# Moving every activation buffer of a two-block transformer kernel 32 bytes down in SBUF

## The reference

```python
def first_block(x, mem, ...):
    memn = rmsnorm(mem, mem_norm)
    for l in range(2):
        h = rmsnorm(x, mix_norm[l])
        x = x + (ab_mixer(h, ...) if l == 0 else c_mixer(h, ...))
        x = x + mem_cross_attn(rmsnorm(x, xa_norm[l]), memn, ...)
        x = x + jnp.square(jax.nn.relu(rmsnorm(x, mlp_norm[l]) @ w1[l])) @ w2[l]
    return rmsnorm(x, final_norm)

def second_block(x, positions, ...):
    for l in range(2):
        h = rmsnorm_2(x, attn_norm[l])
        x = x + (even_attention(h) if l == 0 else moba_attention(h)) @ w_out
        x = x + conv_glu_ffn(rmsnorm_2(x, ffn_norm[l]), ...)
    return rmsnorm_2(x, final_norm)
```

## The kernel before

| buffer | bytes | starts at | modulo 512 |
|---|---|---|---|
| `ring_hi` | 24576 | 0 | 0 |
| `ring` / `ring_lo` | 24576 | 24576 | 0 |
| `consts` | 14636 | 49152 | 0 |
| `smalls` | 6924 | 63808 | 320 |
| `stream_margin` | 352 | 70752 | 96 |
| `xT` | 8192 | 71104 | 448 |

## Time and profile before

### The profile page before, as it was taken

The page is one execution under the profiler, slowest core; times in us unless marked ns, Lnnn a source line. Parts: engine busy times, 40 slices in busy tenths (PEclk is TensorE's granted clock), DMA queues, the critical chain, the costliest instruction groups (busy, mean ns, idle before and its releaser), DMA issues. The chain is left out here.

```text
span 1622.5 us, 32581 instructions
## 1 busy us (share of the span) xinstructions
PE 1558.7 (96%) x12614; PEld 1487.9 (92%) x12614; DVE 730.4 (45%) x1386; ACT 830.8 (51%) x1250; POOL 1183.6 (73%) x920
## 2 busy tenths in 40 slices
PE   7989999999999898999999999999999999999997
PEld 6978989999998788998999998889999997899997
DVE  6554644220187566544422015856553234465511
ACT  5663555554455553545555445465445444654442
POOL 5655966999977500596799897718989896389994
PEclk9999999999999899999999999999999999999999
DMA  7333534555544200353455553415555553255552
GB/s 276 133 104 104 195 118 165 192 195 191 193 166 148 102 1 2 106 194 117 169 193 193 194 189 130 155 47 176 188 189 183 181 195 118 77 172 189 187 183 103
DMA packets 67662, 248.04 MB, mean 153 GB/s; under 512 B 7632, under 2 KB 7888, under 8 KB 67152
## 3 DMA queue, kind: packets, MB, share of 16 engines
q1 hardware_dynamic: 67536, 246.19, 43.7%
HBM read 245.11 MB, written 1.05 MB: 152 GB/s over the span
## 5 line engine op out<-in xcount | busy, mean ns | idle before, releaser
L345 POOL TENSOR_TENSOR ring_lo<-ring,ring_hi 128x512 fp32r<-128x512 f32 x916 | 1183.4, 1330 | 419.6 <-ACT ring_hi L1004 417.4
L1004 ACT ACTIVATE ring_hi<-ring 128x1024 fp32r<-128x1024 f32 x458 | 466.1, 1052 | 200.8 <-DMA ring<-panels 192.7
L379 PE MATMUL ps_dve<-x_hi,ring_hi 128*128 128x256 f32 x1928 | 465.6, 281 | 16.9 <-POOL ring_lo L345 11.0
L379 PE MATMUL ps_dve<-x_lo,ring_hi 128*128 128x256 f32 x1928 | 461.3, 279 | 0.0
L379 PEld LDWEIGHTS ps_dve<-x_hi,ring_hi 128*128 128x128 f32 x1928 | 364.0, 189 | 22.8 <-issue 15.5
L379 PEld LDWEIGHTS ps_dve<-x_lo,ring_hi 128*128 128x128 f32 x1928 | 364.2, 189 | 0.5 <-issue 0.2
L379 PE MATMUL ps_dve<-x_hi,ring_lo 128*128 128x256 f32 x1928 | 274.1, 279 | 0.2
L379 PEld LDWEIGHTS ps_dve<-x_hi,ring_lo 128*128 128x128 f32 x1928 | 246.1, 189 | 0.9 <-POOL ring_lo L345 0.8
L379 PE MATMUL ps_dve<-work_parts,ring_hi 128*128 128x256 f32 x1728 | 228.7, 278 | 0.0
L379 PEld LDWEIGHTS ps_dve<-work_parts,ring_hi 128*128 128x128 f32 x1728 | 214.5, 188 | 0.0
L1492 DVE TENSOR_TENSOR xT<-xT,ps_dve 128x512 f32<-128x512 f32 x40 | 27.5, 687 | 318.9 <-PE ps_dve L379 318.8
(11 more groups left out here) (287 smaller groups left out, 1958.8 us busy)
## 6 DMA issues: line engine op xcount, KB each, us to landing
ring<-panels SPq DMA_DIRECT2D x458, 512.0 KB, 3.4
consts<-constants SPq DMA_DIRECT2D x1, 1700.0 KB, 11.5
xT<-x_t SPq DMA_DIRECT2D x1, 1024.0 KB, 4.9
scratch<-mem_t SPq DMA_DIRECT2D x1, 1024.0 KB, 17.7
out_t<-xT SPq DMA_DIRECT2D x4, 256.0 KB, 2.2
smalls<-small_operands SPq DMA_DIRECT2D x1, 824.5 KB, 14.4
consts<-constants SPq DMA_DIRECT2D x1, 129.5 KB, 4.8
angle_i<-positions SPq DMA_DIRECT2D x1, 128.0 KB, 7.8
```

The source lines that it names most:

```text
L345: pool.tensor_tensor(ring_lo[:, s, cs], ring[:, s, cs], plain(ring_hi[:, s, cs]), ALU.subtract).then_inc(sem("lo_made"), 1)
L379: ins = pe.matmul(o, lhsT, rhs, start=start, stop=stop, skip_group_check=True)
L1004: tell(act.activation(ring_hi[:, n % RING, :], ring[:, n % RING, :], ACT.Copy), "hi_made")
```

## The change

One number. The unused buffer in front of `xT` shrinks from 88 to 80 floats:

```diff
         consts = sb("consts", [P, N_CONST])
         smalls = sb("smalls", [P, N_SMALL])
-        sb("stream_margin", [P, 88])
+        sb("stream_margin", [P, 80])
         xT = sb("xT", [P, C, T])
```

## The result

The changed kernel takes 1655.12 us (median of four runs, 1644.27 to 1662.37) against 1619.43 us for the kernel before (four runs, 1617.06 to 1629.98). The ratio is 1.0194, with a 95% interval of 1.0146 to 1.0243: slower by about 2%, and outside the range of the forecast (1597 to 1645 us).

What follows compares the result with a forecast made beforehand. The prediction took TensorE's matmul count times start-to-start spacing as the bound. All its terms were 0, so 1624.3 us stayed, less 4.3 us for the profiled execution lying above the median: 1620 us, range 1597 to 1645 us.

Steps and rivals of the forecast that it cites:

- What bounds the kernel: TensorE, busy 96% of the span: time is the number of matmuls by their start-to-start distance, plus short waits.
- first effect: Matmul spacing in `project` as operands go from 64 to 96 bytes apart modulo 512: 0 taken, bounded by +22.6 us above.
- A and B: The two start-to-start spacings seen for identical `project` matmuls: about 113.3 ns and about 117.8 ns.
- The argument for 0: In `project`, TensorE's restart decides each stretch's level, and restarts are unchanged by the change, so 0 us.
- second effect: Matmul spacing in `project_tokens`, roles turned round, +64 to +96 bytes: 0 taken, -3.9 us if it reached the faster level.
- third and fourth effect: GpSimd's and other engines' accesses, at most 9 us either way, and single VectorE and ScalarE instructions: 0 us taken.
- All B: Rival: every `project` stretch locks into 117.8 ns at 96 bytes, +22.6 us, 1642.6 us; chance 0.31 including mostly or worse.
- third level above B: Possible slower `project` spacing, one more 4.5 ns step costing another 45 us; nothing showed one; counted within the 0.31.
- A level below A: Rival: `project` matmuls at 109 ns, saving 67 us at most, some 1560 us; chance 0.05.
- One stretch's flip is worth 6.5 us: A long stretch of about 1450 matmuls falling into the other level changes the time by 6.5 us.
- That flips explain the scatter of the runs: One or two long stretches changing level would explain the 11 us between timed runs; the same spread expected after.
- What would show it: Matmul counts in 164 us windows of four long stretches: above 1450 or below 1395 would mean a new level.

Runs made afterwards that it cites:

- `before_again`: The kernel before, unchanged, profiled a second time: 1614.11 us.
- `dist_p64`: The kernel before with only `stream_margin` changed, so activations lie 64 bytes above the ring modulo 512 instead of 64 below: 1648.02 us, ratio 1.0164.
- `one_slot_256`: The kernel before with one of six slots of `ring` and `ring_lo` 256 bytes higher, other distances modulo 512 kept: 1622.39 us, ratio 0.9997.
- `one_slot_96`: The kernel before with one of six slots of `ring` and `ring_lo` 32 bytes higher, its lo matmuls at distance 96: 1616.36 us, ratio 0.9968.

## Why the prediction was wrong

- **What bounds the kernel** was right: the number of matmuls by their distance from start to start. The whole loss is in it, 30 of 29.3 us.
- **The step that failed is the first effect, "TensorE's distance in `project`".** It took the two levels as a property of the engine and the address as something that at most picks between them, with 0 as the value and +22.6 us as the bound from above. In fact the distance sets the levels: at 96 they are 117.3, 118.7 and 120.0 ns, and 113.3 doesn't exist. The measured term is 2.8 ns x 10,000 = +28 us, above the bound. The bound was no bound: the text itself said that no row shows a pair at 96, and then let the rows at 64 and their mirror image stand for it. Every row of `project` had the same distance, so its flips between A and B could show what a start anew does, and nothing of what the distance does.
- **The argument for 0** ("which level a stretch gets depends on how TensorE restarts") was half right. The level is picked anew from start to start, as `before_again` shows, but among levels that the distance allows.
- **`project_tokens`**, second effect: 0 taken, +1.9 us measured (2.3 ns x 830). Its row of 117.8 ns at +64 was the best hint in the trace that the distance matters, and `dist_p64` confirms the reading of it: with the roles turned round, `project` gets 117.8 at +64 too.
- **The other engines**, third and fourth effect: 0 taken, and nothing to be seen.
- **The rivals.** "All B" had the right sign and place, and at 1642.6 us fell 12 short, since after's levels are mostly above B. The third level above B was named and set aside because nothing showed one; it is there. "A level below A" never came at any of the eleven distances, nine of them different modulo 256. Its price was rounded: 67 us off 1620 is 1553 us, not 1560. The 109 ns of the Trainium skill (TensorE: Matmul & The Clock Gate, section "Back-to-back issue gap") that the prediction put beside it is called there the isolated gap of one matmul; the same section says that in a stream with a weight load before each matmul both set the spacing, so it was no figure for this stream.
- **One stretch's flip is worth 6.5 us**: right. FFN 0 takes 176.9 us at 117.8 ns in the first profile and 170.2 at 113.3 in the second. **That flips explain the scatter of the runs** is right in part. Twelve runs lie 27 us apart where the levels are free (`one_slot_256`) and 7 where the slow one is broken (`one_slot_96`), but the granted clock has its share: over the twelve of `one_slot_96` it goes with the time at a correlation of -0.86.
- **What would show it** worked: counts below 1395 in 164 us were named as a new level, with the conclusion that the distance would then set the levels themselves.

## What to carry to other kernels

Where a stream of matmuls is bound by its own pace, read the distance from start to start, not the busy time, and look whether it is the same for identical matmuls. If it isn't, the addresses of the streamed and the stationary operand relative to each other are a variable to scan, in steps of 32 bytes over 256 (here 16 bytes mattered as well, 1.7% and more from the good place): one unused buffer decided over 3%. And a margin that was found good holds only as long as every buffer between the two keeps its size, so it is better to fix the distance than the margin.

## What the runs showed that I had not expected

- Identical matmuls of 256 columns at the full granted clock (1.00, the level of 2.4 GHz) have a spacing of 113.3 to 123.3 ns, and which of these depends on the distance of their two operands modulo 256.
- At some distances two or three levels are stable for 170 us on end, and differ between executions of one program. Eight matmuls at another distance were enough to leave the slow one at 64, four times out of four in the one trace that has them.
- The section of the Trainium skill that the prediction cites (SBUF — State Buffer, "Who interferes with whom") says that PE never waits on anyone and has two independent read ports. As far as other engines go no run speaks against that (GpSimd, ScalarE and VectorE kept their busy times within 2 us from before to after), though none tests it. But TensorE's own two operands are not independent in speed: 113.3 against 120.0 ns.
- Not shown is the mechanism below the levels. That the reads of the next block's weights and of the present columns meet in the same part of the memory fits the period, the mirror image and the slow 0; but no run looked at a single read, and why 48 and 80 are worse than 64 I can't say.
